# Column-half squares at the norms, reordered low parts and one modulation block at the joints of a fused two-block transformer kernel

## The reference

```
# block 1 (one layer)
h = x
h = h + rms_norm(attention(rms_norm(h, g0)), g1)
h = h + rms_norm(relu(rms_norm(h, g2) @ w_up)**2 @ w_down, g3)
# block 2 (two layers); shift, scale, gate come from silu(c) @ ada_w + ada_b
modulate(x) = rms_norm(x) * gain * (1 + scale) + shift
x = x + gate * hgrn2_mixer(modulate(x))        # layer 0, gated linear recurrence
x = x + gate * (silu(a) * b) @ w_out           # a, b = modulate(x) @ w_in
x = x + gate * nsa_mixer(modulate(x), shared)  # layer 1, attention; shared keys from the same x
x = x + gate * (silu(a) * b) @ w_out
rms_norm(x) = x * rsqrt(mean(x*x) + 1e-6)
```

## Time and profile before

| what | value |
|---|---|
| median of 3 runs | 1024.49 us (1023.82 to 1024.69) |
| profiled execution, its own time | 1023.87 us |
| its span | 1022.1 us |
| mean granted TensorE clock | 0.998 of full |
| PE busy | 987.5 us (97%), 5630 matmuls |
| DVE busy | 739.9 us (72%) |
| ACT busy | 510.7 us (50%) |
| POOL busy | 130.1 us (13%) |

### The profile page before, as it was taken

How to read it: one execution, slowest core, us unless ns; L and a number is a source line. 1 busy time by engine, 2 the same in 40 slices (tenths; PEclk the granted TensorE clock), 3 DMA queues, 4 the chain that set the end, 5 groups by cost and what they waited for, 6 DMA issues and landing times.

```text
span 1022.1 us, 15054 instructions
## 1 busy us (share of the span) xinstructions
PE 987.5 (97%) x5630; PEld 811.8 (79%) x5630; DVE 739.9 (72%) x997; ACT 510.7 (50%) x668; POOL 130.1 (13%) x150
## 2 busy tenths in 40 slices
PE   9998999999999998899999999999999999999998
PEld 6777878888887887787778888878878778888886
DVE  4777778676668979896797777989747776545454
ACT  5736365445445576563444343446367635444441
POOL 1000000000002001662410000013911220000000
PEclk9999999999999999999999999999999999999999
DMA  9994359798735979006599989648240337565641
GB/s 352 357 374 176 124 213 379 264 387 287 258 130 203 374 267 346 9 1 206 163 382 336 322 301 337 247 168 272 86 165 3 103 104 254 178 205 164 205 148 57
DMA packets 113650, 227.65 MB, mean 223 GB/s; under 512 B 5024, under 2 KB 58544, under 8 KB 113600
## 3 DMA queue, kind: packets, MB, share of 16 engines
q1 hardware_dynamic: 112048, 222.34, 61.1%
q0 software_dynamic: 1408, 4.54, 1.6%
q10 hardware_dynamic: 144, 0.10, 0.1%
HBM read 225.90 MB, written 1.06 MB: 222 GB/s over the span
## 4 chain that ended last, share of the span: by engine, by line
PE 75%; DVE 13%; DMA 4%; ACT 3%; issue 2%; SPq 1%; POOL 1%; DVEq 0%; ACTq 0%
PE psum L1861 70%; DVE wlo L1201 3%; DVE adaw L1222 2%; DMA raw<-in_attn_w_qkv 1%; DMA raw<-in_hgrn_w_in 1%; PE psum L2448 1%; DMA raw<-in_ffn_w_in 1%; ACT whi L761 1%; PE psum L2305 1%; PE psum L1879 1%; DVE arena L1322 1%; PE psum L2180 1%; DVE arena L1276 1%; DVE gain_b L1557 1%; ACT arena L777 1%
## 5 line engine op out<-in xcount | busy, mean ns | idle before, releaser
L1201 DVE TENSOR_TENSOR wlo<-raw,whi 128x2048 fp32r<-128x2048 f32 (+1 forms) x157 | 311.8, 2003 | 141.9 <-ACT whi L761 141.8
L1861 PE MATMUL psum<-whi,xhi 128*128 128x512 f32 x888 | 351.3, 396 | 5.0 <-DVE xlo L1285 3.3
L1861 PE MATMUL psum<-whi,xlo 128*128 128x512 f32 x888 | 346.2, 390 | 0.0
L1861 PE MATMUL psum<-wlo,xhi 128*128 128x512 f32 x888 | 344.8, 390 | 0.0
L761 ACT CAST whi<-raw 128x2048 fp32r<-128x2048 f32 (+1 forms) x157 | 262.6, 1682 | 164.1 <-PE psum L1861 108.5
L1861 PEld LDWEIGHTS psum<-whi,xhi 128*128 128x128 f32 x888 | 166.8, 188 | 44.0 <-issue 8.4
L1861 PEld LDWEIGHTS psum<-whi,xlo 128*128 128x128 f32 x888 | 166.7, 188 | 35.4
L1861 PEld LDWEIGHTS psum<-wlo,xhi 128*128 128x128 f32 x888 | 166.9, 188 | 32.7
L1222 DVE SCALAR_TENSOR_TENSOR adaw<-adaw,crow 128x1024 f32<-128x1024 f32 x112 | 131.9, 1221 | 0.7 <-DMA adaw<-in_ada_w 0.4
L1861 PE MATMUL psum<-whi,hhi 128*128 128x512 f32 x296 | 115.4, 390 | 0.0
L1861 PE MATMUL psum<-whi,hlo 128*128 128x512 f32 x296 | 115.2, 389 | 0.0
(11 more groups left out here) (271 smaller groups left out, 967.8 us busy)
## 6 DMA issues: line engine op xcount, KB each, us to landing
adaw<-in_ada_w SPq DMA_DIRECT2D x48, 1024.0 KB, 7.5
raw<-in_ffn_w_in SPq DMA_DIRECT2D x88, 512.0 KB
raw<-in_ffn_w_out SPq DMA_DIRECT2D x44, 512.0 KB
raw<-in_w_up SPq DMA_DIRECT2D x16, 1024.0 KB
raw<-in_w_down SPq DMA_DIRECT2D x16, 1024.0 KB
raw<-in_hgrn_w_in SPq DMA_DIRECT2D x16, 1024.0 KB
raw<-in_attn_w_qkv SPq DMA_DIRECT2D x10, 1024.0 KB
adaw<-in_kv_ada_w SPq DMA_DIRECT2D x8, 1024.0 KB, 9.5
```

What stands on the lines that cost most here:

```text
L1201: ve.tensor_tensor(wlo[:, s, 0:width], raw[:, s, 0:width], whi[:, s, 0:width].bitcast(F32), ALU.subtract).then_inc(lo_ready[s], 1)
L1861: return te.matmul(dst, lhsT, rhs, start=start, stop=stop, skip_group_check=open_)
```

## The change

Five edits.

1. The squares that feed a norm are made in column halves of 512, each with a sum of its own, the first as soon as that half is there. This holds for `post` (joints 0 and 1) and for `norm_square` from joint 2 on; those of joints 0 and 1 stay whole. POOL turns each pair of sums into the root with three small instructions (new function `halves`): one after the first half, two after the second; the second one takes both of its scalars from memory. `gained` becomes two instructions of 512 columns.
2. Joint 2: DVE makes slot 1's first low half ahead of tile 0's sum, and the second between the two halves of the sum. Joint 4: slot 1's low part is cut in two; the first is made between the halves of the sum.
3. Joint 3: tile 1's first half is added by DVE, not by POOL.
4. Joint 1: 3 idle matmuls in place of 8 ahead of the transposes. In ACT's and DVE's streams the first half of tile 1's `post` and `gained` stand ahead of tile 0's norm; at joint 0 ACT squares tile 1's first half between the high parts of tile 0.
5. In step 1 of the first gated MLP the first half of the modulation block stands behind the gate product.

```
 # POOL
+            gp.memset(stat[:, 48:49], 1.0 / D)
             def norm(j, i):
-                pool.wait_ge(n_sq, 2 * j + i + 1)
-                rsqrt(ss[:, i:i + 1], rstd[:, i:i + 1], stat[:, 40 + i:41 + i], mhalf[:, 0:1], 1.0 / D, n_rstd)
+                if j < 3:
+                    pool.wait_ge(n_sq, 2 * j + i + 1)
+                    rsqrt(ss[:, i:i + 1], rstd[:, i:i + 1], stat[:, 40 + i:41 + i], mhalf[:, 0:1], 1.0 / D, n_rstd)
+                else:
+                    halves(n_sq, 6 + 4 * (j - 3) + 2 * i, i, 46 + i, 40 + i, rstd[:, i:i + 1], n_rstd)
+            def halves(sq, n, c0, c1, tmp, dst, done):
+                t = stat[:, tmp:tmp + 1]
+                pool.wait_ge(sq, n + 1)
+                chain(gp.tensor_scalar(t, stat[:, c0:c0 + 1], 1.0 / D, EPS, ALU.mult, ALU.add))
+                pool.wait_ge(sq, n + 2)
+                chain(gp.tensor_scalar(t, stat[:, c1:c1 + 1], stat[:, 48:49], t, ALU.mult, ALU.add))
+                gp.tensor_tensor(dst, t, mhalf[:, 0:1], ALU.pow).then_inc(done, 1)
             def post(k, i):
-                pool.wait_ge(p_sq, 2 * k + i + 1)
-                rsqrt(stat[:, 36 + i:37 + i], stat[:, 38 + i:39 + i], stat[:, 42 + i:43 + i], mhalf[:, 0:1], 1.0 / D, p_rstd)
+                halves(p_sq, 4 * k + 2 * i, 36 + i, 44 + i, 42 + i, stat[:, 38 + i:39 + i], p_rstd)
             def tile_added(k):
-                pool.wait_ge(h_gate, k - 1)
+                pool.wait_ge(h_gate, k // 2)
...
-            tile_added(3)
             norms(4)
 # ACT
             def norm_square(j, i):
-                act.wait_ge(p_res, 2 * (j - 1) + i + 1)
-                sc.activation(y[:, i, :], res[:, i, :], ACT.Square, accum_out=ss[:, i:i + 1]).then_inc(n_sq, 1)
+                if j < 3:
+                    act.wait_ge(p_res, 2 * (j - 1) + i + 1)
+                    sc.activation(y[:, i, :], res[:, i, :], ACT.Square, accum_out=ss[:, i:i + 1]).then_inc(n_sq, 1)
+                else:
+                    for f in range(2):
+                        if f:
+                            act.wait_ge(p_res, 2 * (j - 1) + i + 1)
+                        elif i and j != 4:
+                            act.wait_ge(p_add, j // 2)
+                        else:
+                            act.wait_ge(n_half, {3: 1, 4: 2 + i, 5: 4}[j])
+                        c, s = slice(512 * f, 512 * f + 512), (46 if f else 0) + i
+                        sc.activation(y[:, i, c], res[:, i, c], ACT.Square, accum_out=stat[:, s:s + 1]).then_inc(n_sq, 1)
-            def post(k, i):
-                if i == 0:
-                    act.wait_ge(acc_done, k + 1)
-                else:
-                    act.wait_ge(used[3], ACC_END[k] + 1)
-                sc.activation(junk[:, i, :], psum[:, 2 * i:2 * i + 2, :].rearrange("p b n -> p (b n)"), ACT.Square,
-                              accum_out=stat[:, 36 + i:37 + i]).then_inc(p_sq, 1)
+            def post(k, i, f0=0, f1=2):
+                for f in range(f0, f1):
...
+                    s = (44 if f else 36) + i
+                    sc.activation(junk[:, i, 512 * f:512 * f + 512], psum[:, 2 * i + f, :], ACT.Square,
+                                  accum_out=stat[:, s:s + 1]).then_inc(p_sq, 1)
             post(0, 0)
-            norm_high(1, 0)
-            post(0, 1)
+            norm_high(1, 0, stop=2)
+            post(0, 1, 0, 1)
+            norm_high(1, 0, start=2)
+            post(0, 1, 1, 2)
             post(1, 0)
+            post(1, 1, 0, 1)
             norm_square(2, 0)
-            post(1, 1)
+            post(1, 1, 1, 2)
 # DVE
-            def gained(k, i):
+            def gained(k, i, f0=0, f1=2):
...
+                    c = slice(512 * f, 512 * f + 512)
+                    chain(ve.tensor_tensor(y[:, i, c], psum[:, 2 * i + f, :], gain_b[:, c], ALU.mult))
             def residual(k, i, between=None):
                     gated_half(k, i, 0)
-                    added(i, 0, 1)
+                    added(i, 0, 1).then_inc(n_half, 1)
+                    if between is not None:
+                        between()
                     gated_half(k, i, 1)
             residual(1, 0)
+            gained(1, 1, 0, 1)
             norm_scale(2, 0)
-            gained(1, 1)
+            gained(1, 1, 1, 2)
 # DVE, joint 2
-            residual(2, 0)
             split_one(Q_F2A, 0)
-            split_one(Q_F2A, 1)
+            residual(2, 0, lambda: split_one(Q_F2A, 1))
 # DVE, gated MLP
-                if m is not None:
+                if m is not None and not second:
                     ada(m, 1 if end else 0)
                 for i in range(TT):
                     v.wait_ge(act_done, 2 * t + (gb + 16 + i + 1))
                     ve.tensor_tensor(gat[:, i, :], sil[:, i, :], psum[:, (0 if first else 4) + i, 256:512], ALU.mult).then_inc(gate_done, 1)
+                if second:
+                    ada(m, 0)
-            mlp2(1, Q_F2A, HT_F2A, 0, 1 + A_F2A)
+            mlp2(1, Q_F2A, HT_F2A, 0, 1 + A_F2A, second=True)
 # DVE, joint 3
             residual(3, 0)
-            gated_first(3)
+            gated_half(3, 1, 0)
+            added(1, 0, 1).then_inc(n_half, 1)
             gated_half(3, 1, 1)
             norm_scale(4, 0)
-            v.wait_ge(p_add, 2)
             added(1, 1, 2).then_inc(p_res, 1)
 # DVE, joint 4
-            residual(4, 0)
-            split(1, Q_F2B)
+            residual(4, 0, lambda: split_one(Q_F2B, 0))
+            split_one(Q_F2B, 1)
             norm_scale(5, 0)
 # PE, joint 1
-            project_tiles(Q_HIN, 2, 2, 8)
+            project_tiles(Q_HIN, 2, 2, 3)
```

More of the change, by code:

```diff
@@ L315, in build @@
         gate_row = sem("gate_row")
-        h_gate, p_add = sem("h_gate"), sem("p_add")
+        h_gate, p_add, n_half = sem("h_gate"), sem("p_add"), sem("n_half")
         a_qk, a_qks, a_s, a_m, a_e, a_pt, a_pts, a_o, a_os = [sem("a_" + s) for s in ("qk", "qks", "s", "m", "e", "pt", "pts", "o", "os")]
@@ L784, in norm_high @@
                     sc.copy(xhi[:, 2 * q:2 * q + 2 * pairs, c], xf[:, 2 * q:2 * q + 2 * pairs, c]).then_inc(n_hi, pairs)
-            def post(k, i):
-                if i == 0:
-                    act.wait_ge(acc_done, k + 1)
-                else:
-                    act.wait_ge(used[3], ACC_END[k] + 1)
-                sc.activation(junk[:, i, :], psum[:, 2 * i:2 * i + 2, :].rearrange("p b n -> p (b n)"), ACT.Square,
-                              accum_out=stat[:, 36 + i:37 + i]).then_inc(p_sq, 1)
+            def post(k, i, f0=0, f1=2):
+                for f in range(f0, f1):
+                    if f == 0:
+                        act.wait_ge(acc_half, 2 * k + i + 1)
+                    elif i == 0:
+                        act.wait_ge(acc_done, k + 1)
+                    else:
+                        act.wait_ge(used[3], ACC_END[k] + 1)
+                    s = (44 if f else 36) + i
+                    sc.activation(junk[:, i, 512 * f:512 * f + 512], psum[:, 2 * i + f, :], ACT.Square,
+                                  accum_out=stat[:, s:s + 1]).then_inc(p_sq, 1)
             def turn_high(k, b):
@@ L1242, in norm_scale @@
                 v.wait_ge(n_rstd, 2 * j + i + 1)
-                v.wait_ge(n_sq, 2 * j + i + 1)
+                v.wait_ge(n_sq, 2 * j + i + 1 if j < 3 else 6 + 4 * (j - 3) + 2 * i + 2)
                 ve.tensor_scalar(y[:, i, :], res[:, i, :], rstd[:, i:i + 1], None, ALU.mult).then_inc(n_y, 1)
@@ L1299, in evac @@
                 ve.tensor_copy(dst, psum[:, 2 * p + 1, 0:dst.shape[-1]]).then_inc(evac_d, 1)
-            def gained(k, i):
+            def gained(k, i, f0=0, f1=2):
                 v.wait_ge(gain_in, 16 * k + 16)
[L1304 to L1310, removed]
+                for f in range(f0, f1):
+                    if f == 0:
+                        v.wait_ge(acc_half, 2 * k + i + 1)
+                    elif i == 0:
+                        v.wait_ge(acc_done, k + 1)
+                    else:
+                        v.wait_ge(used[3], ACC_END[k] + 1)
+                    v.wait_ge(p_sq, 4 * k + 2 * i + f + 1)
+                    c = slice(512 * f, 512 * f + 512)
+                    chain(ve.tensor_tensor(y[:, i, c], psum[:, 2 * i + f, :], gain_b[:, c], ALU.mult))
             def gated_half(k, i, f, slot=3, done=None):
@@ L1341, in gated_first, with residual @@
                 gated_half(k, 1, 0, done=h_gate)
-            def residual(k, i):
+            def residual(k, i, between=None):
                 if k < 2:
@@ L1612, in joint @@
                 low(k, 0, 1)
-                v.wait_ge(p_add, j - 2)
+                v.wait_ge(p_add, j // 2)
                 added(1, 1, 2).then_inc(p_res, 1)
@@ L1624, in _, with mlp2 @@
             joint(3, 3)
-            def mlp2(t, q0, hb, gb, m=None, first=False, nxt=2048, last=False, end=False):
+            def mlp2(t, q0, hb, gb, m=None, first=False, nxt=2048, last=False, end=False, second=False):
                 if m is not None and end:
```

## The result

The changed kernel takes 1015.79 us (median of 4 runs, 1014.18 to 1018.1) against 1024.47 for the kernel before on the same chip: ratio 0.9923, 95% interval 0.9911 to 0.9935. In a later run it was 0.9927 (0.9914 to 0.9939). The gain is 8.7 us where 6.3 were forecast: the direction is right, and the time is 1.0 us under the low end of the range.

What follows compares the result with a forecast made beforehand. PE, busy 97% of the span, was taken as the bound, with gains only where it waits, mainly at the joints. Terms summed to 6.29 us, taking the median from 1024.49 to 1018.2, range 1016.8 to 1021.5.

Steps and rivals of the forecast that it cites:

- rival A: Loads behind joint 1 don't move, so gains of joints 0 and 1 and step 1 are lost: 2.46 us, 1020.7; chance 0.15.
- Joint 0: DVE's two half multiplies start at once instead of waiting for ACT's whole square: 0.53 us.
- Joint 1: Shorter squares and multiplies, reordered halves and fewer idle matmuls let DVE's scale and shift start sooner: 0.98 us for PE.
- Joint 2, tile 0: POOL no longer held by DVE's low parts, and a half square on the path: 1.15 us of PE's idle 1.35.
- Joint 4, tile 0: Second low half shortened, so POOL is held less long behind the sum: 1.10 us of PE's idle 1.30.
- Tile 1: At joints 2 and 4, low parts end sooner and scaling needn't wait for the root: 0.34 us at each.
- Joint 3: POOL's add goes to DVE, so root and scaling come sooner; POOL's first step held by that add: 0.90 us.
- Step 1: First gated MLP: gate product ahead of modulation ends PE's 1.49 us stall; 0.95 stays, the rest becomes a wait for slot 1.
- rival B: PE's clock falls at joint 1 with only three idle matmuls, costing 1.7 us: 1019.9; chance 0.05.
- C: POOL stays held at joints 2 to 4 by other DVE work: 3.15 us lost, 1021.3; chance 0.08.
- D: POOL's new two-scalar instruction is dear at eight roots; from 0.88 us extra each the kernel is slower; chance 0.04.

Runs made afterwards that it cites:

- e5: Changed kernel with eight idle matmuls in place of three ahead of joint 1's transposes: 1018.14 us, ratio 0.9944 to the kernel before.
- e11: Changed kernel with DVE's low parts of slot 1 put back behind tile 0's sum at joints 2 and 4: 1018.71 us, ratio 0.994.
- e12: Kernel before with only the modulation block of the gated MLP's step 1 put behind the gate product: 1022.78 us, ratio 0.9987.
- e8: Kernel before with the edits of joints 2, 3 and 4 alone: 1020.34 us, ratio 0.9968.
- e6: Kernel before with three idle matmuls in place of eight at joint 1: 1021.75 us, ratio 0.9976.
- e4: Kernel before with eleven idle matmuls as filler in PE's stand near 404 us: 1022.4 us, ratio 0.9987.
- e2: Changed kernel, unchanged, measured and profiled a second time: 1015.81 us, ratio 0.9927 to the kernel before.
- e7: Changed kernel with ten empty instructions ahead of joint 1's idle matmuls; none show in the profile, so taken as the changed kernel again: 1015.31 us, ratio 0.9914.

## Why the prediction fell short

The main step that failed is in rival A: the stretch from joint 1 to 404 us, in which nothing was changed, was taken as one that could only keep or lose what was gained ahead of it, and the sum has no term for it. It became 1.4 us shorter. First the terms that the sum does have, point by point.

- **Joint 0** (0.53 forecast): 0.61; DVE's two half multiplies run together (127.81 to 129.22) with no wait for ACT. (The 0.53 compares the halves' end with the start of the next instruction, 128.59; end against end, 127.32 + 1.23 = 128.55, it would have been 0.49.) **Joint 1** (0.98): 0.89. The three idle matmuls left PE 0.35 idle. The reason given for taking five out was over-priced: eight would have cost 0.3 (e5), not "all of it".
- **Joint 2, tile 0** (1.15): 0.95. PE still stands 0.39 where the 1.35 less 1.15 left 0.2. The pointer step, taken at 0.19, costs 0.34 (0.33 was the nearest row): that is 0.15 of the 0.20 missing. The mechanism is right: e11 shows that POOL's hold is what the joint lost.
- **Joint 4, tile 0** (1.10): 0.90, for the same reason (0.41). **Tile 1** at both (0.34): 0.31.
- **Joint 3** (0.90): 0.76. The forecast held POOL's first step; held were both (0.53 and 0.61). It ended near the tie, not at the 0.4 of both held in full.
- **Step 1** (0.95): 1.06; alone 1.1 by the medians (e12; 0.4 to 2.3 by the interval). The new wait is there, 0.36 in place of 0.5. In e12's profile slot 1's load landed sooner, the new wait is under 0.2 and PE gains 1.4: how much of the 1.49 comes is set by that load's landing.
- The joints and step 1 together: 5.79 against 6.29. Joints 2 to 4 alone measured 3.2 (e8) where the trace shows 3.23.

So every term of the sum held within 0.2, and by the sum alone the median would have been 1018.7. What failed are two steps around it, and each left out a possible gain.

**Rival A's argument,** "every load behind joint 1 is asked for by work behind it and moves along". The loads were indeed issued 0.18 sooner and no gain was given back. But the argument took the landing as a fixed time behind the issue. Removing five matmuls moved a code packet by 0.9 us against one load and took away the late part of that load. It was worth 1.37 in the traces, 1.8 by the medians of e6; the prediction had listed no way in which that stretch could become shorter. Its own test, the stretch from 330 to 404 beginning sooner and ending at the same time, came out the other way: the stretch began 0.2 sooner, and PE's stand at its end was over 1.5 sooner.

**The fall of PE's clock behind 404 us** was read in the earlier trace rows and used to price rival B, but its end was not among the possible gains. In the kernel before it was there in every profile without filler, and filler at that place takes 1.5 us off. In the changed kernel PE's stand there fell from 3.5 to 2.1 with the earlier landing, and half of its runs show no fall of the clock at all, so its median holds only a part of that price. The forecast's price for a fall, 1.7 us, is near what the runs show (1.5 by e4, 1.6 by e2 and e7).

The account of the median: 5.8 from the joints and step 1, 1.4 from slot 1's load, and the remaining 1.5 of 8.7 (0.9 of 8.1 in the second measurement) is of the size of one clock fall (1.6 between e2 and e7), which the kernel before shows in both of its profiles, while half of the changed kernel's runs are without any fall. Runs at one clock bear this out as far as they go: the kernel before has a single run at 1.000, 1022.18, and on the same chip the middle one of e7's three at 1.000 is 1014.99. That is 7.2 less, the 5.8 and the 1.4 without the fall. The start, which varies by 1.0 between profiles, is in the remainder too. That the median lies as low as it does is therefore in part a matter of how many of its runs had the fall.

The rivals: B didn't happen (the granted clock is 1.00 from 300 to 320 us in e6 and e7, with three idle matmuls). C is refuted by POOL's rows, and e11 shows what it would have cost. D was the right item at the wrong size: the pointer step costs 0.15 more than the other form, not 0.88.

What remains open: which engine's program the packet belongs to (that it moves with PE's matmuls points to PE's), and why one transfer engine stays late. In both kernels the last part of each of the seven loads that follow, up to 369 us, is marked behind the other 15, by 1.6 us in the kernel before and 1.2 in the changed one. So the changed kernel has its late part too, from the next load on; there ACT doesn't wait for it. The direct test, a shift of the program by instructions that do nothing, is missing, since e7 shows no shift.

## What to carry to other kernels

Where a load lands late by one part of sixteen, look in the transfer queues for a packet of the instruction queue in the microsecond before: here its place moved with the number of matmuls in the program, so that an edit 230 us upstream, in idle time, created the wait again. Before a sum is made, list the waits in the stretches that the change doesn't touch and ask of each whether it could also get shorter; a clock fall behind a stand is such a price, and can be worth a filler (1023.9 to 1022.4 in the kernel before; in the changed one no gain clear of the noise). On GpSimd's path between a sum and a root, keep VectorE off differences of two SBUF tiles: putting 2.3 us of them back behind the sum cost 1.0 us at each of two joints, and with them there the halved squares gained nothing. What moving them gives without the halved squares wasn't measured.

## What the runs showed of the hardware that was not expected

- A 16,384-byte packet of the instruction queue takes 1.07 to 1.09 us amid a full queue, and one of the 16 parts of the load lands 1.3 to 1.6 us behind the other 15 in all seven profiles with the packet 0.7 to 1.0 us ahead of the first landing mark; with the packet 0.0 to 0.3 us behind that mark, all 16 parts land within 0.5 us, in all seven others.
- A GpSimd instruction of one column with both scalars from memory takes 0.34 us against 0.19 for the form with constants, and 1.47 (e11) when VectorE subtracts SBUF tiles beside it.
- PE's granted clock fell to the 1.2 GHz level behind the stand near 404 us in all six profiles where it was 3.3 to 3.5 us long, and in four of the five where it was 2.0 to 2.15; with the filler, in none of three. One fall cost 1.6 us between two profiles of one program.
